# Attention on one core: the order of turns and value products within a half chunk

## What is computed

```python
def _sink_attend(q, k, v, sinks, valid):
    s = jnp.einsum('bqhgd,bkhd->bhgqk', q, k).astype(jnp.float32) * (HD ** -0.5)
    ...
    m = jnp.maximum(jnp.max(s, axis=-1, keepdims=True), sink)
    p = jnp.exp(s - m)
    p = p / (jnp.sum(p, axis=-1, keepdims=True) + jnp.exp(sink - m))
    return jnp.einsum('bhgqk,bkhd->bqhgd', p.astype(v.dtype), v)
```

## Time and profile before

| | |
|---|---|
| median of three timed runs | 5150.5 us |
| the profiled execution: time, span | 5139.61 us, 5138.3 us |
| attention stage, from the scores of chunk 3 to the last output turns | 2866.42 to 3162.50, 296.08 us |
| TensorE busy in that stretch | 257.81 us |
| mean granted TensorE clock there, and over the whole span | 0.52, 0.92 |

### The profile page before, as it was taken

One profiled execution on the slowest core, in us unless ns is written; L12 is line 12 of the kernel. 1 busy time (PEld: TensorE's weight loads), 2 busy tenths in 40 slices (PEclk: granted clock), 3 DMA queues, 4 the chain that ended last, 5 costly groups with the idle time before them and its releaser, 6 DMA issues. The chain is left out here.

```text
span 5138.3 us, 94405 instructions
## 1 busy us (share of the span) xinstructions
PE 4537.8 (88%) x38337; PEld 4273.2 (83%) x38337; DVE 1878.8 (37%) x2917; ACT 1621.6 (32%) x3026; POOL 976.7 (19%) x863
## 2 busy tenths in 40 slices
PE   5899997999887899979859788669999999999994
PEld 4789997888787899979836566669999999999993
DVE  3455404666522100011122322234445454455554
ACT  2573212333322000022200322334344444444442
POOL 0334323444332222313200001310000000000001
PEclk6899998999999899999979656889999999999997
DMA  1222225454242222134120000275556666676675
GB/s 43 63 67 89 93 89 123 99 118 99 59 139 63 75 71 63 59 107 121 56 58 14 1 0 26 75 198 158 158 160 176 173 186 176 171 202 179 177 208 197
DMA packets 975328, 563.49 MB, mean 110 GB/s; under 512 B 139201, under 2 KB 941346, under 8 KB 975090
## 3 DMA queue, kind: packets, MB, share of 16 engines
q1 hardware_dynamic: 909570, 486.33, 34.2%
q10 hardware_dynamic: 55344, 46.60, 3.2%
q0 software_dynamic: 10176, 27.19, 1.9%
HBM read 481.79 MB, written 77.93 MB: 109 GB/s over the span
## 5 line engine op out<-in xcount | busy, mean ns | idle before, releaser
L2220 DVE TENSOR_TENSOR experts_w_lo<-experts_raw,experts_w_hi 128x1024 fp32r<-128x1024 f32 x352 | 415.9, 1222 | 157.5 <-ACT experts_w_hi L2152 157.5
L209 PE MATMUL experts_pa<-experts_hx,experts_w_hi 128*128 128x272 f32 (+5 forms) x1408 | 410.4, 291 | 8.3 <-DVE experts_w_lo L2220 8.3
L209 PE MATMUL experts_pd<-experts_hid,experts_w_hi 128*128 128x272 f32 (+5 forms) x1408 | 411.2, 292 | 0.0
L209 PE MATMUL experts_pb<-experts_hx,experts_w_hi 128*128 128x272 f32 (+5 forms) x1408 | 408.2, 290 | 3.1 <-DVE experts_w_lo L2220 3.1
L210 PE MATMUL experts_pa<-experts_hx,experts_w_hi 128*128 128x272 f32 (+5 forms) x1408 | 408.7, 290 | 0.0
L211 PE MATMUL experts_pa<-experts_hx,experts_w_lo 128*128 128x272 f32 (+5 forms) x1408 | 408.7, 290 | 0.0
L211 PE MATMUL experts_pd<-experts_hid,experts_w_lo 128*128 128x272 f32 (+5 forms) x1408 | 407.9, 290 | 0.0
L210 PE MATMUL experts_pd<-experts_hid,experts_w_hi 128*128 128x272 f32 (+5 forms) x1408 | 407.7, 290 | 0.0
L210 PE MATMUL experts_pb<-experts_hx,experts_w_hi 128*128 128x272 f32 (+5 forms) x1408 | 407.5, 289 | 0.0
L211 PE MATMUL experts_pb<-experts_hx,experts_w_lo 128*128 128x272 f32 (+5 forms) x1408 | 407.5, 289 | 0.0
L209 PE MATMUL proj_pm<-hT,proj_w_hi 128*128 128x384 f32 (+1 forms) x1152 | 386.4, 335 | 14.6 <-POOL proj_w_lo L527 14.6
(11 more groups left out here) (398 smaller groups left out, 11196.2 us busy)
## 6 DMA issues: line engine op xcount, KB each, us to landing
experts_raw<-in_moe_w SPq DMA_DIRECT2D x352, 512.0 KB, 4.7
experts_raw<-in_moe_w SPq DMA_DIRECT2D x128, 704.0 KB, 5.9
projected<-proj_out SPq DMA_DIRECT2D x48, 544.0 KB, 3.7
proj_w<-in_gdn_w_in ACTq DMA_DIRECT2D x48, 512.0 KB, 4.1
ffnup_w<-in_ffn_w SPq DMA_DIRECT2D x44, 512.0 KB, 5.0
ffndown_w<-in_ffn_w SPq DMA_DIRECT2D x32, 704.0 KB, 4.7
mixout_w<-in_gdn_w_out SPq DMA_DIRECT2D x32, 512.0 KB, 4.0
delta_kkq<-projected SPq DMA_DIRECT2D x102, 128.0 KB, 2.9
```

What stands on the lines that cost most here:

```text
L209: pe.matmul(out, as_r(w_hi), as_r(x_hi), start=first, stop=False)
L2220: dve.tensor_tensor(as_r(w_lo[:, x, 0:KD, :]), raw[:, x, 0:KD, :], w_hi[:, x, 0:KD, :], ALU.subtract).then_inc(split[x], 1)
```

## The change

Within each half, the four turns over 128 keys now stand first and the four over 64 keys behind them; likewise the four value products over 128 keys stand first and the four over 64 keys behind them. The waits and the signals stay at their places. The start flag, which was set on the first product of each of the four pieces, is now set on the first product of a half only; the 64-key products still add to the 128-key products.

```diff
@@ -1596,24 +1596,26 @@
                     pe.wait_ge(e["exped"], PRE + 2 * i + jp + 1)
                     pe.wait_ge(e["p_copied_a"], PRE + 2 * i + jp)
                     pe.wait_ge(e["p_copied_b"], PRE + 2 * i + jp)
-                    for x in range(4):
-                        p = prob[:, 2 * jp + x // 2, x % 2, :]
-                        if v0 is not None:
-                            last = pe.transpose(pt[:, 0, x, :], p[:, 0:P], ident)
-                        if v1 is not None:
-                            last = pe.transpose(pt[0:CHUNK, 1, x, :], p[:, keys - CHUNK:keys], ident)
+                    p = lambda x: prob[:, 2 * jp + x // 2, x % 2, :]
+                    if v0 is not None:
+                        for x in range(4):
+                            last = pe.transpose(pt[:, 0, x, :], p(x)[:, 0:P], ident)
+                    if v1 is not None:
+                        for x in range(4):
+                            last = pe.transpose(pt[0:CHUNK, 1, x, :], p(x)[:, keys - CHUNK:keys], ident)
                     last.then_inc(e["p_turned"], 1)
                     pe.wait_ge(e["v_staged"], PRE + i + 1)
                     pe.wait_ge(e["p_copied_a"], PRE + 2 * i + jp + 1)
                     pe.wait_ge(e["p_copied_b"], PRE + 2 * i + jp + 1)
                     pe.wait_ge(e["o_normed"], PRE + 2 * i + jp)
-                    for x in range(4):
+                    whole, half = v0 is not None, v1 is not None
+                    for x in range(4 if whole else 0):
                         j = 2 * jp + x // 2
-                        pieces = [(pT[:, 0, x, :], vs[:, par, 0, j * HD:(j + 1) * HD])] if v0 is not None else []
-                        if v1 is not None:
-                            pieces.append((pT[0:CHUNK, 1, x, :], vs[0:CHUNK, par, 1, j * HD:(j + 1) * HD]))
-                        for n, (l, r) in enumerate(pieces):
-                            last = pe.matmul(po[:, j, x % 2, :], l, r, start=(n == 0), stop=(n == len(pieces) - 1))
+                        last = pe.matmul(po[:, j, x % 2, :], pT[:, 0, x, :], vs[:, par, 0, j * HD:(j + 1) * HD], start=(x == 0), stop=not half, skip_group_check=True)
+                    for x in range(4 if half else 0):
+                        j = 2 * jp + x // 2
+                        last = pe.matmul(po[:, j, x % 2, :], pT[0:CHUNK, 1, x, :], vs[0:CHUNK, par, 1, j * HD:(j + 1) * HD],
+                                         start=not whole and x == 0, stop=True, skip_group_check=True)
                     last.then_inc(e["pv_summed"], 1)
 
                 def body(i, par):
```

## The result

The changed kernel takes 5078.95 us (median of four runs, 5074.94 to 5083.81) against 5149.89 for the kernel before in the same set (four runs, 5143.58 to 5151.6): a ratio of 0.9865, 95% interval 0.9848 to 0.9882.

What follows compares the result with a forecast made beforehand. The attention stage was taken as one chain along TensorE; its products over 30 halves were to fall from 142.6 to 100.6 us, a gain of 42.0, so 5150.5 - 42 = 5108.5, predicted as 5108, range 5090 to 5123.

Steps and rivals of the forecast that it cites:

- What bounds the stage: Attention stage: one chain along TensorE, including its waits for copies; what TensorE saves between waits comes off the span.
- The price of a change of row count: Value products: each switch between 128 and 64 rows costs 0.19 us at low clock, 0.146 at high; six removed a half.
- The unknown pitch of 128-row products at the low clock: Value products: time per 128-row pass at 1.2 GHz, bounded by 0.215 and 0.304 us, taken as 0.215.
- same: Value products: the excess belongs to going on to another product or output part, so time stays 5150.5; chance 3%.
- slower: Second product group: each pass waits for earlier results to land, 15 us slower, 5165; chance 2%.
- turns gain: Turns: six fewer column changes at 0.19 us in 30 halves save 34 us more, 5074; chance 1%.
- The count of high halves: Attention stage: 10 of 30 halves with products at the high clock, bounds none and 20; gain 42.0 us.
- The price of a high half: Value products: about 2.4 us for a half at the high clock, 2.13 + (3.28 - 3.00).
- a few us more: Attention stage: additional gain, beyond 56.3 us with 20 high halves, for turns that fall under the high clock.
- The base: Whole kernel: 5150.5 us, the timed median, 10.9 above the profiled execution, carried over to the forecast.
- The range: Whole kernel: 5090 to 5123 us, its ends set by 20 and by no high halves; this case has 85%.
- The clock rival: Attention stage: denser chunks keep TensorE at 2.4 GHz in 25 of 30 halves, gain 63 us, 5080; chance 7%.

Runs made afterwards that it cites:

- the pairs: Products ordered 128, 128, 64, 64, 128, 128, 64, 64 rows, three row-count changes a half against seven in the kernel before: 5097.17 us, ratio 0.9915.
- the lengthened kernels: Kernel before with one, two or all four output turns of a chunk repeated, or second-half outputs scaled twice: 5142.4, 5125.63, 5139.66 and 5136.31 us.
- the filled kernels: Kernel before and changed kernel, each with unread identity turns in TensorE's waits for copies and scaled outputs: 5072.16 and 5032.81 us.

## Why the prediction was right and wrong

*What bounds the stage* was right: the waits for copies are as many and as long as before. Of the 63.0 us off the stretch 55.8 came off the span of the profiled execution; 6.3 of the rest are a later start of the stretch, which lies ahead of the change, and 0.9 lie behind it.

*The price of a change of row count* was right to 0.03 us a half: 3.84 against 3.83 at the low clock, 2.10 against 2.13 at the high one, 4.22 and 2.39 with three changes. Six changes at 1.32/7 are 1.13 us and not 1.15, so its own terms give 3.85. The 0.146 at the high clock came from a half of 3.00 us that was not high to its end (its last record takes 0.32 us, where its like take 0.27); a half that was takes 2.95, and (2.95 - 2.11)/6, like (2.39 - 2.11)/2 from the pairs, is 0.14. The unknown pitch of 128-row products at the low clock is 0.21 (eight in 1.94). The turns cost nothing, by a kernel of their own. The rivals "same", "slower" and "turns gain" fall with these rows.

*The count of high halves* was the step that failed. I took 10 of 30, from the rate in the first ten halves of the kernel before, and said it was a choice. It was 19 in both profiled executions. In the sum of products that is worth 9 x (3.83 - 2.4) = 12.9 us of the 18.2 between forecast (100.6) and measurement (82.4). The reasoning that a chunk of another length behaves otherwise was borne out by the lengthened kernels; but I had no row that tells how often such a chunk rises, and the ten early halves were no rate for it. The kernel with only the turns grouped has the same 20.40 us chunk, was low from its second half to its 17th and then had three high ones running (3.48, 3.01 and 3.39 us): where the rises fall in the stage is not fixed, and being early is not their cause. Nor was the repetition broken in the changed kernel; it settled into a row of six chunks with seven of twelve halves high. A count of 20 stood in the text, as the end of the range and not as likely. Why the row is this one stays open: the runs show that the count changes when a chunk is only made longer, by work or by a wait, and that it does not simply grow with the length.

*The price of a high half* was the second step that failed: I carried over 0.28 us for products that outlast the high clock, from the earlier trace rows. Grouped products are short enough to end before the clock falls, 2.11 each in 17 of 19 and at most 2.18: 19 x 0.28 = 5.3 us. So fewer changes gain twice: the products are shorter, and the whole group fits under the high clock. The products are 60.2 us of the stretch's 63.0; the remaining 2.8 fit turns that caught some of the high clock (0.67 in place of 1.06 above; "a few us more" in the text), and were not added up.

*The base.* I took 10.9 us between the profiled execution and the median of three runs as an offset to carry over. The profiled execution of the kernel before had the earliest start of the stretch of all fourteen (2865 us), so part of this offset can lie ahead of the stage. Three later sets of the kernel before have medians of 5142.61 to 5145.06, so 5150.5 was at the upper side. From 5150.5 the stretch's 63 give 5087.5, already below the range. The other 8.5 us down to 5078.95 are not traced to a row: within the set the medians differ by 70.9 us, against the later sets by 64 to 66, and what lies ahead of the stretch and behind it varies by 11 and 8 us from execution to execution. That part of the miss may be chance.

*The range* went wrong by treating 20 high halves at the price of a partly high one as its end. With 20 at 2.11, plus the turns, from the same base its end would have been about 5085, still 6 us above the measured time. The clock rival (25 of 30 high, 5080) came near the measured time with a count that was too high: luck.

## What to carry to other kernels

Products that use different numbers of rows should stand in groups: with 64 columns a pass, as here, a change costs about as much as a pass. Where TensorE hops between the two clock levels, price a change at both, and take the share of high stretches as the largest unknown of the sum: here it changed when the repeating piece was only made longer, so that even added work made a kernel faster. The steady way out in this kernel was to keep TensorE busy in its short waits: then the products of 28 of 30 halves of the changed kernel took 2.07 to 2.11 us.

## What the runs showed of the hardware

A change from 128 to 64 rows or back costs 0.19 us at 1.2 GHz and 0.14 at 2.4 GHz beside a pass of 0.213 and 0.112, in either direction; a change between 128 and 64 columns at 128 rows costs nothing that shows (ratio 1.0002, 0.9992 to 1.0011). TensorE stood at 1.2 GHz for most of a stage in which it was busy for 257.35 of 296.02 us and none of its repeated waits was longer than 1.2 us; with turns of the identity in these waits the mean granted clock went from 0.52 to 0.89 and from 0.64 to 0.94. The Trainium skill (TensorE: Matmul & The Clock Gate, Part 4) says that the higher clock does not engage for turns; the filled kernels disagree, since their fillers are turns and six of them took 0.82 us at the high clock, 1.49 at the low one. And a pattern of the clock can repeat for many chunks: 20.40 us with no half high, 17.05 with one of two, 17.07 with both in part or whole, and the six chunks of the changed kernel.
